# Feed-forward activations and memory outputs 128 bytes further in SBUF

## The chip, the core and the metric

The kernel runs on one core of a Trainium2 chip. The metric is the device time of one execution in microseconds, as the median of several runs. The traces show one profiled execution each.

## What is computed

A sequence of 256 tokens with 1024 features goes through two layers of one kind and one layer of another. All of it is in float32.

```
for l in range(2):                                   # first kind
    h = hybrid_mixer(x, ...)                         # three branches, gated, merged, @ w_mix_out
    x = layer_norm(alpha * x + h, ...)
    h = memory_cross_attention(x, mem, ...)          # softmax(q k) v, then  o @ xa_o
    x = layer_norm(alpha * x + h, ...)
    u, gt = split(x @ ffn_w_in)                      # 1024 -> 2 x 2816
    h = (silu(dwconv(gt, w) + b) * u) @ ffn_w_out    # 2816 -> 1024
    x = layer_norm(alpha * x + h, ...)
# second kind, once
x = x + rms_norm(merged @ w_o)
h = rms_norm(x)
z = conv_b + causal_conv(h @ w_up)                   # both halves, 3 taps
x = x + rms_norm((silu(gate) * val) @ w_down)
```

## The kernel before

Every dense product is done with three matmuls in a 32-bit format with shortened mantissa (`F32R`). A value is split into a high part and the rest: hi x hi, hi x lo and lo x hi are added up in PSUM. So each activation and each weight lies in SBUF twice, as `..._hi` and `..._lo`.

**Weights** come as one stream of 525 halves of 128 x 1024 floats. A half is loaded by DMA into a ring of 5 (`raw_weights`). The scalar or vector engine copies it into `weights_hi` (ring of 4 halves), and the vector engine makes `weights_lo` as the difference (lines 1166 and 1622). A half holds four tiles of 256 columns. TensorE waits for `weights_lo` of a half before it uses it.

**Matmuls.** `linear` (line 601) goes over `kcs` chunks of 128 features. For each chunk it issues six matmuls: two halves of the output by the three products of parts. It has two shapes. With `feature_major` (line 621) the 128 x 128 tile loaded into the array is a weight tile, and the activations, 256 columns, stream. Without it (line 625) the loaded tile is 128 tokens of the activations, and 256 columns of weights stream. Each matmul has a weight load of its own (rows with LDWEIGHTS), which runs beside the matmul ahead of it.

**Feed-forward.** `ffn` (line 964) goes over 11 pairs of feature chunks. For each pair it makes "gt" and "up" (two calls of `linear` with `xT`, line 621, 96 matmuls together), and then, one pair behind, `down_product` (line 639, matmuls in line 663): 48 matmuls in which a tile of `ffn_act` is loaded and 256 columns of the weights stream. They add up over all pairs in four PSUM banks whose names in the trace are `scores`, `probs_transposed` and `attention_out`. The order on TensorE is gt and up of pair 0 and 1, product 0, pair 2, product 1, and so on, then product 9 and product 10. The order is written out by hand; all engines follow it with semaphores. The vector engine writes `ffn_act_hi` and `ffn_act_lo` (lines 1989 and 1632) once per pair, into two slots in turn.

**Memory outputs.** `memory_out` (`XO`) holds the heads' outputs of the cross attention for the product with `xa_o` (line 1059 and 1061, shape of line 625: 4 calls in each of the two layers). The last layer uses the same place for its normalised low-rank inputs (lines 1103 to 1107), streamed 3 x 4 and 2 x 2 chunks, loaded in 24 matmuls.

**Places in SBUF.** One arena is cut by hand; `place` holds the start of each part. `attention_area` is one part in which tiles of different stages overlap. Added up from the sizes in the list, in bytes from the arena's start: weight halves begin at multiples of 4096, `xT_hi` at 70080, `memT_hi` at 102848, `attention_area` at 163136. Each chunk of an activation is 1024 bytes long, each loaded tile 512 bytes. `SHIFT` is 32 floats, 128 bytes. Modulo 512 the weight tiles are on 0, and `xT`, `memT` and `second_branch` on 448. `first_branch`, `third_branch` and `merged`, which have `SHIFT` in their place, are on 448 too (`merged` on 960 modulo 1024), and `ffn_act` and `memory_out`, which do not, on 320.

Of the kernel before, what the change touches and what calls it, by code (L numbers as in the profile page):

```python
# [22 lines left out]
F32R = mybir.dt.float32r  # L23
# [6 lines left out]
T = 256  # L30
# [19 lines left out]
SHIFT = 32  # L50
# [186 lines left out]
def build(nc, a, out):  # L237
    stage = Stage()
    ctx = ExitStack()
    with ctx:  # L240
# [21 lines left out]
        def sb(name, cols, where=None, col0=0, dt=F32):  # L262

            return nc.alloc_sbuf_tensor_at(name, [P, cols], dt, offset=place[where or name] + 4 * col0)
# [16 lines left out]
        area = sb("attention_area", 48 * T + SHIFT, "area")  # L281
        ya_hi, ya_lo = (sb(f"first_branch_{k}", 4 * T, "area", c + SHIFT, F32R) for k, c in (("hi", 0), ("lo", 4 * T)))
        yc_hi, yc_lo = (sb(f"third_branch_{k}", 4 * T, "area", c + SHIFT, F32R) for k, c in (("hi", 28 * T), ("lo", 32 * T)))
        fa_hi, fa_lo = (sb(f"ffn_act_{k}", 4 * T, "area", c, F32R) for k, c in (("hi", 0), ("lo", 4 * T)))
        mg_hi, mg_lo = (sb(f"merged_{k}", 8 * T, "area", c + 128 + SHIFT, F32R) for k, c in (("hi", 8 * T), ("lo", 16 * T)))
        xo_hi, xo_lo = (sb(f"memory_out_{k}", 8 * T, "area", c, F32R) for k, c in (("hi", 24 * T), ("lo", 32 * T)))
        rows = area[:, 40 * T + SHIFT:48 * T + SHIFT]
        stat = sb("softmax_stats", 24, "stat")
        nst = sb("norm_stats", 112, "nst")
# [2261 lines left out]
```

## Time and profile before

| what | value |
|---|---|
| median of 3 runs | 1636.07 us (1635.97 to 1636.3) |
| span of the profiled execution, first to last instruction | 1634.2 us |
| TensorE busy, matmuls | 1620.2 us in 13642 |
| vector engine busy | 1155.2 us |
| scalar engine busy | 868.8 us |
| data moved by DMA | 305.85 MB, 187 GB/s on the mean |
| matmuls of line 621 with `xT` | 3 x 2432 |
| matmuls of line 663 with `ffn_act` | 3 x 528 |
| matmuls of line 625 with `memory_out` | 3 x 136 |

How to read it: matmuls overlap in the array, so one that lasts 276 ns starts about 113 ns after the one before it. The busy time says that TensorE has always something in flight; the rate is read from starts, or from the chain of work, which lists merged runs with their length. The granted TensorE clock is at its upper level, 2.4 GHz, through the whole span.

### The profile page before, as it was taken

Reading aid. Unit: us, or ns where it says so; the run is one execution under the profiler, and the core shown is the slowest. Engines: PE = TensorE matmul, PEld = TensorE weight load, DVE = VectorE, ACT = ScalarE, POOL = GpSimd, SP = SyncE. Lnnn points to the kernel's source line nnn. Section 1 sums busy time; section 2 is a strip of 40 time slices with the busy share of each in tenths; the row PEclk is TensorE's granted clock in tenths of the full one; section 3 lists DMA queues with packets and bytes.
Section 4 is the critical chain, followed back from the end, with each engine's and each line's share of the span. In section 5 each row is a group of like instructions: output and inputs, shape, how many; then the busy total and the mean of one; then the engine's idle time right before and its main releaser. Section 6 shows DMA issues by size and latency. Waiting matters only on the chain.

```text
span 1634.2 us, 32191 instructions
## 1 busy us (share of the span) xinstructions
PE 1620.2 (99%) x13642; PEld 1584.0 (97%) x13642; DVE 1155.2 (71%) x1730; ACT 868.8 (53%) x1305; POOL 40.5 (2%) x59
## 2 busy tenths in 40 slices
PE   9999999999999999999999999999999999999998
PEld 9999999999999999999999999999999999999998
DVE  6588778658666767977974866568576545877777
ACT  5456544646444454555355644455755555464554
POOL 3030000000000000000000000000000000000000
PEclk9999999999999999999999999999999999999999
DMA  9984456535656564445564465655454453556562
GB/s 313 305 213 155 149 197 248 194 130 187 209 173 206 168 238 168 161 149 188 201 234 160 151 227 178 207 173 186 163 173 168 155 180 132 192 168 207 173 204 102
DMA packets 83071, 305.85 MB, mean 187 GB/s; under 512 B 10704, under 2 KB 10832, under 8 KB 80752
## 3 DMA queue, kind: packets, MB, share of 16 engines
q1 hardware_dynamic: 77280, 279.44, 50.1%
q0 software_dynamic: 5648, 24.35, 5.0%
q8 instruction: 108, 1.77, 0.4%
q14 instruction: 35, 0.29, 0.1%
HBM read 300.52 MB, written 6.29 MB: 188 GB/s over the span
## 4 chain that ended last, share of the span: by engine, by line
PE 90%; DVE 7%; issue 1%; ACT 1%; DMA 0%; SPq 0%; DVEq 0%; ACTq 0%
PE general L621 56%; PE general L625 14%; PE scores L663 5%; PE attention_out L663 3%; PE probs_transposed L663 3%; DVE weights_lo L1622 2%; PE attention_out L815 2%; PE scores L748 1%; PE probs_transposed L767 1%; PE scores L839 1%; ACT weights_hi L1166 1%; DVE x_tok L1696 1%; DVE x_tok L1693 1%; DVE xT_lo_part L1632 1%; PE attention_out L859 1%
## 5 line engine op out<-in xcount | busy, mean ns | idle before, releaser
L1622 DVE TENSOR_TENSOR weights_lo<-raw_weights,weights_hi 128x1024 fp32r<-128x1024 f32 x525 | 633.4, 1222 | 372.0 <-ACT weights_hi L1166 369.4
L1166 ACT ACTIVATE weights_hi<-raw_weights 128x1024 fp32r<-128x1024 f32 x525 | 553.2, 1058 | 390.6 <-PE general L621 219.0
L621 PE MATMUL general<-xT_hi_part,weights_hi 128*128 128x256 f32 x2432 | 683.4, 281 | 2.3 <-DVE weights_lo L1622 2.0
L621 PE MATMUL general<-xT_lo_part,weights_hi 128*128 128x256 f32 x2432 | 674.8, 277 | 0.0
L621 PE MATMUL general<-xT_hi_part,weights_lo 128*128 128x256 f32 x2432 | 674.7, 277 | 0.0
L621 PEld LDWEIGHTS general<-xT_hi_part,weights_hi 128*128 128x128 f32 x2432 | 457.4, 188 | 10.5 <-issue 8.8
L621 PEld LDWEIGHTS general<-xT_lo_part,weights_hi 128*128 128x128 f32 x2432 | 457.2, 188 | 1.4 <-issue 1.0
L621 PEld LDWEIGHTS general<-xT_hi_part,weights_lo 128*128 128x128 f32 x2432 | 458.0, 188 | 0.0
L1965 DVE SCALAR_TENSOR_TENSOR exp_ring<-general,param_cols,exp_ring 128x255 f32<-128x255 f32 (+1 forms) x176 | 76.8, 478 | 46.2 <-ACT exp_ring L1362 44.7
L1362 ACT ACTIVATE exp_ring<-general,param_cols 128x256 f32<-128x256 f32 x88 | 44.9, 561 | 69.6 <-PE general L621 69.6
L625 PE MATMUL general<-weights_hi,xT_hi_part 128*128 128x256 f32 x272 | 76.6, 281 | 0.0
L625 PE MATMUL general<-weights_hi,xT_lo_part 128*128 128x256 f32 x272 | 75.8, 279 | 0.0
L625 PE MATMUL general<-weights_lo,xT_hi_part 128*128 128x256 f32 x272 | 75.7, 278 | 0.0
L663 PE MATMUL scores<-weights_hi,ffn_act_hi 128*128 128x256 f32 x264 | 74.1, 281 | 0.8 <-DVE weights_lo L1622 0.8
L663 PE MATMUL scores<-weights_lo,ffn_act_hi 128*128 128x256 f32 x264 | 74.2, 281 | 0.0
L663 PE MATMUL scores<-weights_hi,ffn_act_lo 128*128 128x256 f32 x264 | 74.2, 281 | 0.0
L1177 ACT ACTIVATE attention_area<-general 128x512 f32<-128x512 f32 x60 | 35.7, 595 | 66.4 <-PE general L621 44.1
L1222 ACT ACTIVATE exp_ring<-exp_ring,softmax_stats 128x256 f32<-128x256 f32 (+2 forms) x56 | 28.9, 517 | 67.5 <-DVE softmax_stats L1811 67.4
L625 PEld LDWEIGHTS general<-weights_hi,xT_hi_part 128*128 128x128 f32 x272 | 51.0, 188 | 0.2 <-DVE xT_lo_part L1654 0.2
L1222 ACT ACTIVATE exp_ring<-scores,softmax_stats 128x256 f32<-128x256 f32 x56 | 26.0, 471 | 47.2 <-DVE softmax_stats L1811 47.2
L625 PEld LDWEIGHTS general<-weights_lo,xT_hi_part 128*128 128x128 f32 x272 | 51.1, 188 | 0.0
L625 PEld LDWEIGHTS general<-weights_hi,xT_lo_part 128*128 128x128 f32 x272 | 51.0, 188 | 0.0
(328 smaller groups left out, 2947.4 us busy)
## 6 DMA issues: line engine op xcount, KB each, us to landing
raw_weights<-in_stream SPq DMA_DIRECT2D x525, 512.0 KB, 4.2
attention_area<-in_ln_rows POOLq DMA_DIRECT2D x9, 1024.0 KB, 5.2
bias_scratch<-in_rpb POOLq DMA_DIRECT2D x32, 96.0 KB, 10.5
attention_area<-bias_scratch POOLq DMA_DIRECT2D x2, 1536.0 KB, 8.9
memT_hi<-memT_scratch POOLq DMA_DIRECT2D x2, 1024.0 KB, 5.0
memT_lo<-memT_scratch POOLq DMA_DIRECT2D x2, 1024.0 KB, 8.8
attention_area<-in_mem SPq DMA_DIRECT2D x2, 512.0 KB, 6.0
z_tok<-in_x SPq DMA_DIRECT2D x1, 1024.0 KB, 10.5
```

What stands on the lines that cost most here:

```text
L621: ins = nc.tensor.matmul(ps[b][0:m, half * T:half * T + T], w[wk][:, half * m:half * m + m], x[xk_], start=first, stop=last, skip_group_ch ...
L625: ins = nc.tensor.matmul(ps[b][:, half * T:half * T + T], x[wk][:, half * P:half * P + P], w[xk_], start=first, stop=last, skip_group_chec ...
L663: ins = nc.tensor.matmul(down[2 * t + c][:, q * TILE_N:q * TILE_N + TILE_N], act[xk_][:, kc, t * P:t * P + P], w[wk][:, at:at + TILE_N], s ...
L748: ins = nc.tensor.matmul(dst[:, lo:hi], q, k, start=(c == 0), stop=(c == len(pairs) - 1))
L767: ins = nc.tensor.transpose(tp[:, kt * T + t * P:kt * T + t * P + P], e[:, kt * P:kt * P + P], ident)
L815: ins = nc.tensor.matmul(po[r0:r0 + m, c * T + lo:c * T + T], v, p[:, lo:T], start=first, stop=(g == parts - 1 and kt == 1))
L1166: nc.scalar.activation(hi_half(h), raw_half(h), ACT.Copy).then_inc(*hi_done.more())
L1177: nc.scalar.activation(dst, src[:, :].rearrange("p (c w) -> p c w", w=T), func, **kw).then_inc(*read(key))
L1222: ins = nc.scalar.activation(e, src, ACT.Exp, bias=st("nm", j, t, t + 1), scale=scale if name not in ("na", "mla") else 1.0, accum_out=st( ...
L1362: ins = nc.scalar.activation(cbuf(i % 2, k)[:, c * T:c * T + T], src[:, c * T:c * T + T], ACT.Identity, bias=colp(b, ch, packed), scale=co ...
L1622: nc.vector.tensor_tensor(lo_half(h), raw_half(h), hi_half(h).bitcast(F32), ALU.subtract).then_inc(*lo_done.more())
L1965: ins = nc.vector.scalar_tensor_tensor(d, s, colp(w, 3 * ch + tap, packed), d, ALU.mult, ALU.add)
```

## The change

Two pairs of tiles get `SHIFT` added to their column in `attention_area`: `ffn_act_hi` and `ffn_act_lo`, and `memory_out_hi` and `memory_out_lo`. No instruction, wait or transfer is added, removed or moved. Modulo 512 both pairs are then on 448. `ffn_act` ends 128 bytes further, still ahead of `merged`, and `memory_out` ends where `rows` begins.

```diff
-        fa_hi, fa_lo = (sb(f"ffn_act_{k}", 4 * T, "area", c, F32R) for k, c in (("hi", 0), ("lo", 4 * T)))
+        fa_hi, fa_lo = (sb(f"ffn_act_{k}", 4 * T, "area", c + SHIFT, F32R) for k, c in (("hi", 0), ("lo", 4 * T)))
         mg_hi, mg_lo = (sb(f"merged_{k}", 8 * T, "area", c + 128 + SHIFT, F32R) for k, c in (("hi", 8 * T), ("lo", 16 * T)))
-        xo_hi, xo_lo = (sb(f"memory_out_{k}", 8 * T, "area", c, F32R) for k, c in (("hi", 24 * T), ("lo", 32 * T)))
+        xo_hi, xo_lo = (sb(f"memory_out_{k}", 8 * T, "area", c + SHIFT, F32R) for k, c in (("hi", 24 * T), ("lo", 32 * T)))
```

## Rows read from the trace of the kernel before

**Rows 1.** The page: span, busy time of the engines, engines' shares of the chain.

```profile
span 1634.2 us, 32191 instructions
...
PE 1620.2 (99%) x13642; PEld 1584.0 (97%) x13642; DVE 1155.2 (71%) x1730; ACT 868.8 (53%) x1305; POOL 40.5 (2%) x59
...
PE 90%; DVE 7%; issue 1%; ACT 1%; DMA 0%; SPq 0%; DVEq 0%; ACTq 0%
```

**Rows 2.** Groups of matmuls: streamed tile, loaded tile, count | busy us, mean ns.

```profile
L621 PE MATMUL general<-xT_hi_part,weights_hi 128*128 128x256 f32 x2432 | 683.4, 281 | 2.3 <-DVE weights_lo L1622 2.0
...
L625 PE MATMUL general<-weights_hi,xT_lo_part 128*128 128x256 f32 x272 | 75.8, 279 | 0.0
...
L663 PE MATMUL scores<-weights_hi,ffn_act_lo 128*128 128x256 f32 x264 | 74.2, 281 | 0.0
...
L625 PE MATMUL general<-weights_hi,merged_hi 128*128 128x256 f32 x176 | 48.6, 276 | 0.0
...
L625 PE MATMUL general<-weights_hi,memory_out_lo 128*128 128x256 f32 x136 | 37.7, 277 | 0.0
```

**Rows 3.** Waits of TensorE in the whole run: total us, times, longest.

```profile
PE general L621 <- DVE weights_lo L1622: 2.6, 5, 1.0
```

**Rows 4.** Chain in order of time, one product and block: start us, length us, count.

```profile
425.38 1.41 PE scores L663 x12
426.80 0.71 PE probs_transposed L663 x6
427.50 0.71 PE attention_out L663 x6
428.21 10.90 PE general L621 x96
```

**Rows 5.** Chain in order of time, entry into the first down product.

```profile
394.89 11.11 PE general L621 x98
406.00 1.41 PE scores L663 x12
```

**Rows 6.** Matmuls with `ffn_act_hi` from 1623.5 us: duration ns min/median/max, first, last.

```profile
L663 PE MATMUL scores<-weights_hi,ffn_act_hi x7: 276/276/279, 1623.4 to 1625.5; 128*128 128x256 f32 x7
...
L663 PE MATMUL attention_out<-weights_hi,ffn_act_hi x4: 276/276/276, 1627.2 to 1628.2; 128*128 128x256 f32 x4
```

**Rows 7.** Chain in order of time, other changes from line 621 to 625.

```profile
1185.98 0.91 PE general L621 x8
1186.88 2.83 PE general L625 x24
...
257.91 5.56 PE general L621 x49
263.47 24.49 PE general L625 x216
...
35.98 22.26 PE general L621 x189
58.24 10.83 PE general L625 x92
```

**Rows 8.** Chain in order of time, changes from line 625 to 621.

```profile
354.94 15.64 PE general L625 x138
370.58 2.84 PE general L621 x24
...
1317.08 5.66 PE general L625 x48
1322.74 5.47 PE general L621 x48
...
1133.24 12.98 PE general L625 x108
1146.22 18.84 PE general L621 x160
```

**Rows 9.** Vector engine in order of time: a write of `ffn_act_lo`; start us, length us.

```profile
421.08 0.69 DVE L1632 TENSOR_TENSOR ffn_act_lo<-exp_ring,ffn_act_hi 128x512 fp32r<-128x512 f32 x1
```

## The prediction

> **What bounds the kernel now.** I read the page first: TensorE is busy 1620.2 of 1634.2 us, and it carries 90% of the chain that ended last [rows 1]. Then its waits: in the whole run the largest releaser, the vector engine's `weights_lo`, costs the products of line 621 2.6 us in five waits [rows 3], and the wait view of the first feed-forward stretch (405 to 566 us) names nobody that TensorE waited for. So inside the feed-forward stage the time is the number of matmuls times the spacing between two of them, and no weight or activation comes late. Every matmul there has its own weight load, which runs beside the matmul ahead of it.
>
> The spacing has two values. The chain lists merged runs of matmuls with start and length, so length over count is the spacing. Inside a feed-forward block the 96 matmuls of "gate" and "up" take 10.90 us, 113.5 ns each; the 48 of a down product take 2 x 1.41 + 4 x 0.71 = 5.66 us, 117.9 ns each [rows 4]. I call them fast and slow; the difference is 4.4 ns. The mean duration in the groups shows the same by another number: 276 ns in a fast stretch, 281 in a slow one. Down products against `ffn_act` have 281, projections against `merged` 276, and `memory_out` 277 [rows 2].
>
> I use two shapes below. **F** (line 621): the activations stream and the weights are loaded. **K** (lines 625, 663, 955): the weights stream and the activations are loaded. Offsets are bytes modulo 512 from the arena's start, added up from the sizes: weight halves 0, `xT`, `memT`, branches and `merged` 448, `ffn_act` and `memory_out` 320.
>
> **Does the offset make it slow?** Not alone. The last down product of the run, after its wait, has a median of 276 ns with `ffn_act` at 320 [rows 6]. And K with `xT` at 448 has a mean of 279 [rows 2], and 48 such matmuls from 1317.08 us take 5.66 us, the slow spacing, with the target offset [rows 8]. Fast and slow are states: once in one, a stretch of one shape stays in it over dozens or hundreds of matmuls, and it changes at a wait or at a change of shape. So I look at changes of shape without a wait.
> - Fast F into K at 320: slow. 11.11 us for 98 (113.4 ns), then 1.41 for 12 (117.5) [rows 5]. All 30 entries into the down products look so. `memory_out`, streamed and then loaded, also goes from 0.91 us for 8 (113.8) to 2.83 for 24 (117.9) [rows 7].
> - Fast F into K at 448: stays fast. Branches into `merged`: 5.56 us for 49, then 24.49 for 216, both 113.4 [rows 7]; three such places. Slow F into K at 448 stays slow: 22.26 us for 189 (117.8), then 10.83 for 92 (117.7) [rows 7]; two places.
> - Slow K at 320 into F: fast, at all 27 places between down products and the next block [rows 4].
> - Fast K into F: slow. 15.64 us for 138 (113.3), then 2.84 for 24 (118.3) [rows 8]; both places where it occurs, with `memory_out` loaded ahead and `memT` (448, as `xT`) streamed after.
> - Slow K at 448 into F: fast at three places, the 48 of 1317.08 us followed by 48 in 5.47 us (114.0) as the shown one; at one it stays slow: 12.98 us for 108, then 18.84 for 160 (117.8) [rows 8].
>
> **The change, part by part.** It adds, removes and moves no instruction, wait or transfer; three tile addresses change their base by 128 bytes. The vector and scalar engines write the same shapes; I cost that at nothing, since the vector engine is idle 29% of the span and nothing on TensorE's side waits for it inside the stage. The writes of `ffn_act` end about 0.6 us before their product starts (421.08 + 0.69 us against 422.4) [rows 9], so 128 bytes either way would have to lengthen a write by half before TensorE waits; a slower block only widens that gap.
>
> Down products. A block order is: gate and up of pairs 0 and 1, product 0, block 2, product 1, ..., block 10, products 9 and 10. Today, per layer, the 11 products are slow (528 matmuls) and all blocks after the first are fast. After the change product 0 is entered from a fast block and should stay fast (branches into `merged`). Then comes the step that matters: leaving a fast K. The weight load of the next block then runs beside a matmul at the fast timing, as in rows 8, and there the F stretch went slow. So block 2 is slow, product 1 stays slow (rows 7), and leaving it gives fast again (3 of 4). The pattern has a period of two blocks: of 288 matmuls 144 are slow, against 96 now. Counted out per layer: slow blocks after products 0, 2, 4, 6, 8 (5 x 96 = 480) and slow products 1, 3, 5, 7, 9, 10 (6 x 48 = 288), 768 in place of 528. 240 x 3 layers x 4.4 ns = 3.2 us longer.
>
> Memory outputs. They are loaded in 408 matmuls of line 625 in all. At 277 in place of 276 ns about one in five is slow now. After restarts K at 448 is mostly slow (mean 279 against `xT`, [rows 2]); if `memory_out` becomes like that, 3 in 5, some 160 to 200 more are slow, 0.7 to 0.9 us; the two groups of 48 that follow the output projections without a wait would then go from slow to fast, 0.4 back. Net 0.5, between 0 (nothing changes) and 1.4 (all slow). The 96 matmuls that stream `memory_out` in the last block cannot hold more than 0.4 either way.
>
> Sum: 3.2 + 0.5 = 3.7 us on a span of 1634.2. What lies around the span, 1.9 us (median 1636.1 less span), stays. **1639.8 us.**
>
> What the Trainium skill says on this ("SBUF — State Buffer", section Operand start alignment): an operand only has to begin at a multiple of its element size, and the page adds that its runs timed nothing. By it alone 320 and 448 would be alike; that is case E below. The spacing itself, by "TensorE: Matmul & The Clock Gate" (section Back-to-back issue gap), is set by the weight load and the matmul together; the rows agree so far as the two states differ in this pair, 113.5 and 117.9 ns, but that page has nothing about two states or addresses.
>
> **The rivals.**
> - B, faster: the F stretch after a fast product stays fast. Its place is the 27 exits from down products, and it decides there alone: for it speaks that no exit from a fast K at 448 into F is in the trace (after the projections against `merged` comes another K), and that both fast exits seen are from 320. Against it: at that moment the loaded tile is a weight half at offset 0 and no activation is loaded any more, so the 448 should not matter. Then nearly all of the 1584 product matmuls turn fast; some 40 at the end already are: 1540 x 4.4 ns = 6.8 us less, with memory outputs 0.5 more: 1629.8.
> - C, no difference: `ffn_act` is entered slow at 448 too. For it: the entry from `memory_out` to itself had equal offsets and went slow, and `ffn_act` against `xT` would have equal offsets as well; `merged` differs from the branches by 512 bytes. Exits stay as today. Only the 0.5 stays: 1636.6.
> - D, slower still: exits from a slow K at 448 keep the slow state (1 in 4). Then all nine blocks after product 0 are slow too: 9 x 96 x 3 = 2592 matmuls x 4.4 ns = 11.4 us, 1648.
> - E, the change does not do what it says: the states have nothing to do with the offset, and it comes out at 1636.1.
>
> **How the numbers follow.** A 0.38, B 0.24, C 0.20, D 0.09, E 0.09. A mixture, with some exits that stay slow, would lie between A and D. The range takes in A, B, C, E with the bounds of the memory outputs and leaves D: 1628.5 to 1644. A's own range is 1638.2 (only two thirds of the blocks, memory 0) to 1644. What a measurement can tell from no change is about 0.2%, 3.3 us, so faster means below 1632.8 and slower above 1639.3. Faster: B, 0.24. Same: C, E and the low end of A, 0.20 + 0.09 + 0.05 = 0.34. Slower: the rest of A and D, 0.42.
>
> **What would show it.** In the groups, `ffn_act` matmuls split between 276 and 281 ns with a mean near 278 to 279 (A), all 276 (B), all 281 (C, D). In the chain of one layer, blocks of 96 that alternate between 10.9 and 11.3 us (A), all 10.9 (B, C), all 11.3 (D). The mean of `xT` in line 621 should rise by about 1 ns in A, as 1440 of its 7296 matmuls turn slow. The first product of each layer tells the entry step, the block behind it the exit step. TensorE's waits should be as now; if instead its waits for `weights_lo` grow, the supply of weights had no room for the faster stage and B's gain is smaller. What would make the prediction wrong is mainly the exit step, which rests on two places, and an entry step that rests on three with another distance between the tiles.

## The result

The changed kernel takes 1638.72 us (median of 21 runs, 1637.21 to 1640.01) against 1636.07 (21 runs, 1632.55 to 1637.75): ratio 1.0017, 95% interval 1.001 to 1.0023. It is slower by 2.7 us; the interval leaves out 1, so the direction stands. The forecast was 1639.8, slower by 3.7. By the forecast's own limit for calling a kernel slower, 1639.3 us, the result still counts as no change. The profiled execution has a span of 1637.5 us, 3.3 more than before.

The page of the changed kernel, the lines that answer to [rows 1]:

```profile
span 1637.5 us, 32191 instructions
...
PE 1622.9 (99%) x13642; PEld 1586.6 (97%) x13642; DVE 1155.8 (71%) x1730; ACT 869.2 (53%) x1305; POOL 40.6 (2%) x59
```

The groups that answer to [rows 2]: `xT` in line 621, `ffn_act`, `merged`, `memory_out`.

```profile
L621 PE MATMUL general<-xT_lo_part,weights_hi 128*128 128x256 f32 x2432 | 676.7, 278 | 0.0
L663 PE MATMUL scores<-weights_hi,ffn_act_lo 128*128 128x256 f32 x264 | 73.3, 278 | 0.0
L625 PE MATMUL general<-weights_hi,merged_lo 128*128 128x256 f32 x176 | 48.6, 276 | 0.0
L625 PE MATMUL general<-weights_hi,memory_out_lo 128*128 128x256 f32 x136 | 37.9, 279 | 0.0
```

`ffn_act` went from 281 to 278 ns: the products became faster, as the offset seems to promise. `xT` in the blocks between them rose (277 to 278 over 2432 matmuls of this kind), `memory_out` from 277 to 279, `merged` did not move. The chain in order of time, layer 0, two rounds of product and block, answering to [rows 4] (start us, length us, count):

```profile
429.03 11.31 PE general L621 x96
...
445.99 10.89 PE general L621 x96
456.89 1.36 PE scores L663 x12
458.25 0.68 PE probs_transposed L663 x6
458.93 0.68 PE attention_out L663 x6
459.61 1.36 PE scores L663 x12
460.97 0.68 PE probs_transposed L663 x6
461.65 0.68 PE attention_out L663 x6
462.33 11.31 PE general L621 x96
473.64 1.42 PE scores L663 x12
```

The block at 445.99 us is fast (113.4 ns), so is the product behind it (2 x 1.36 + 4 x 0.68 = 5.44 us, 113.3 ns), the next block is slow (11.31 us, 117.8 ns) and the product behind that too. This is the period of two blocks from the forecast. Read block by block from starts of matmuls, every block and product of all three layers follows it, but for one exit in layer 1 that stayed slow: the one behind that layer's first product, at 960.20 us.

### The profile page after: what moved, and what is told of

It reads as the page before. It is cut to its first block, busy times and chain, and to the rows that moved or that the text cites. A ratio compares the mean times of both kernels' runs of the same rounds, so it can differ in the third digit from the quotient of the medians.

```text
span 1637.5 us, 32191 instructions
## 1 busy us (share of the span) xinstructions
PE 1622.9 (99%) x13642; PEld 1586.6 (97%) x13642; DVE 1155.8 (71%) x1730; ACT 869.2 (53%) x1305; POOL 40.6 (2%) x59
## 4 chain that ended last, share of the span: by engine, by line
PE 89%; DVE 7%; ACT 2%; issue 1%; DMA 0%; SPq 0%; DVEq 0%; ACTq 0%
PE general L621 56%; PE general L625 14%; PE scores L663 5%; PE attention_out L663 2%; PE probs_transposed L663 2%; DVE weights_lo L1622 2%; PE attention_out L815 2%; PE scores L748 1%; PE probs_transposed L767 1%; ACT weights_hi L1166 1%; PE scores L839 1%; DVE x_tok L1696 1%; DVE x_tok L1693 1%; DVE xT_lo_part L1632 1%; PE attention_out L859 1%
```

## The experiments

Each kernel was compared with the kernel before on the same chip. "Fast" and "slow" are the 113.4 and 117.8 ns spacings, F streams activations (line 621), K loads them (lines 625 and 663). Offsets are from the arena's start. In e3 to e12 `memory_out` stays on 320.

**Each half of the change alone.**

```diff
 # e1_ffn_only
-        fa_hi, fa_lo = (... "area", c, F32R) ...
+        fa_hi, fa_lo = (... "area", c + SHIFT, F32R) ...
 # e2_mem_only
-        xo_hi, xo_lo = (... "area", c, F32R) ...
+        xo_hi, xo_lo = (... "area", c + SHIFT, F32R) ...
```

> Only ffn_act moves by 128 bytes, memory_out stays on 320. Theory (states pass through the change of shape; a product at 448 keeps the state it is entered in, leaving a fast product makes the next block slow, leaving a slow one makes it fast): the feed-forward blocks alternate as in the changed kernel, chain rows of 96 matmuls at 10.9 and 11.3 us in turn, ffn_act mean 278 ns, about +3 us against the kernel before, so nearly all of the change's loss. Rival (the loss comes from memory_out and from the stages behind it): under +1 us.

Measured: 1638.01 us, ratio 1.0012 (1.0003 to 1.0021); the medians lie 1.6 us apart, the ratio says 2.0. The alternation is there, chain of its trace:

```profile
428.19 11.31 PE general L621 x96
...
445.16 10.89 PE general L621 x96
456.05 1.36 PE scores L663 x12
```

> Only memory_out moves, ffn_act stays on 320. Theory: feed-forward as before (ffn_act 281 ns, blocks of 96 all 10.9 us), memory_out 279 ns in place of 277, between 0 and +1.4 us. Rival (memory_out carries the loss): +2 us or more.

Measured: 1636.43 us, ratio 1.0004 (0.9995 to 1.0013). `memory_out` has 279 ns, the products keep 281:

```profile
L663 PE MATMUL scores<-weights_hi,ffn_act_lo 128*128 128x256 f32 x264 | 74.1, 281 | 0.0
L625 PE MATMUL general<-weights_hi,memory_out_lo 128*128 128x256 f32 x136 | 37.9, 279 | 0.0
```

So most of the loss is the feed-forward stage, and the memory outputs add what cannot be told from zero. The traces say the same: from the first to the last matmul of line 663 the three stages together are 2.3 us longer than before in e1, as in the changed kernel, and equal to before within 0.01 us each in e2. The 279 ns alone prove little for `memory_out`: it has the same mean in e3, e4 and e12, where it was not moved. Here too the other half of the forecast's term shows: the 24 matmuls behind the last output projection take 2.75 us (114.6 ns) in place of 2.84 [rows 8], since leaving a slow K gives a fast F.

**How far the offset counts.**

```diff
 # e3_ffn_plus512: 320 modulo 512, 832 modulo 1024
+        fa_hi, fa_lo = (... "area", c + 4 * SHIFT, F32R) ...
 # e4_ffn_plus640: 448 modulo 512, 960 modulo 1024, as merged
+        fa_hi, fa_lo = (... "area", c + 5 * SHIFT, F32R) ...
 # e8_ffn64: 64 modulo 512
+        fa_hi, fa_lo = (... "area", c + 2 * SHIFT, F32R) ...
```

> ffn_act moves by 512 bytes: still 320 modulo 512, but another offset modulo 1024. If only the offset modulo 512 counts: all products slow, all blocks behind them fast, the time of the kernel before within 0.5 us. If the period is longer (1024 or more), entries or exits differ from before and the stage shows another pattern.

> ffn_act moves by 640 bytes: 448 modulo 512 and 960 modulo 1024, exactly where merged lies. If only modulo 512 counts: the alternation of the changed kernel, about +3 us. If modulo 1024 counts: another pattern, up to all fast (-7 us) should the exit from 960 keep the fast state.

> Only ffn_act moves, to 64 modulo 512 (256 bytes further than before). Theory: entry at distance 64 turns slow or keeps slow, exits from slow products turn fast, so the pattern and time of the kernel before (0 to +0.5 us). Rival (320 is the one bad offset): alternation as with 448, +3 us.

Measured: e3 1637.01 us, ratio 1.0005 (0.9995 to 1.0014); e4 1638.88, ratio 1.0017 (1.0008 to 1.0026); e8 one run of 1635.88 beside a median of 1635.88. The chains of e3, e4 and e8, in this order:

```profile
429.02 10.90 PE general L621 x96
439.93 1.41 PE scores L663 x12
```

```profile
428.03 10.89 PE general L621 x96
438.93 1.36 PE scores L663 x12
```

```profile
428.18 10.90 PE general L621 x96
439.08 1.41 PE scores L663 x12
```

At 320 and 832 a fast block is followed by a slow product (1.41), at 448 and 960 by a fast one (1.36). And 64 behaves as 320. So for the loaded activation the offsets that were tried fall into two classes modulo 256: 64 (offsets 64, 320, 832) and 192 (offsets 448, 960). My rival of a longer period falls, and "320 is the one bad offset" falls too.

**Moving what streams.** I held that the distance of loaded and streamed tile decides. The next kernels move `xT` instead. Its two tiles go behind everything else, with a gap that sets the offset; all other tiles keep theirs modulo 512.

```diff
-                 ("x", 2 * D), ("z", 2 * D), ("xT_hi", 2 * D), ("xT_lo", 2 * D), ("keep", 2 * D), ("big", 24 * T),
+                 ("x", 2 * D), ("z", 2 * D), ("keep", 2 * D), ("big", 24 * T),
-                 ("stat", 24))
+                 ("stat", 24), ("gap", 8), ("xT_hi", 2 * D), ("xT_lo", 2 * D))
```

The gap is 8 floats for `xT` on 64 and 24 for 128. The expectation of e10 says 0 modulo 512, but its gap of 56 is 192 bytes more than that of e5, so `xT` lies on 256 modulo 512, which is 0 modulo 256. `ffn_act` has `+ SHIFT` in e5, e9 and e10 (448), nothing in e6 (320), `+ 2 * SHIFT` in e7 (64).

> xT_hi and xT_lo lie behind everything else, on 64 modulo 512 in place of 448; ffn_act on 448; all other tiles keep their offset modulo 512. Theory (what counts is the distance loaded minus streamed: at 448, as with merged, a disturbed start falls back to the fast state, at 320 and 64 it turns slow): streaming xT at 64 with weights loaded at 0 has the distance 448, so leaving a fast product leaves the next block fast. All blocks of 96 at 10.9 us, and if the entry holds too all products at 5.4 us; -7 us or more, since other stretches with xT (7296 matmuls, 2000 slow before) turn fast as well. Rival (only the absolute offset of the loaded activation counts): blocks alternate as in the first experiment, +3 us.

> xT on 64, ffn_act on 320 as before. Theory: blocks all fast; the entry into the products has the distance 320 and turns slow or, if the exit and entry distances matter in another way, not: products 281 ns, about the kernel before or some us less by the other stretches with xT. Rival (offset of xT without effect): the kernel before within 0.1%.

> xT on 64, ffn_act on 64. Theory: in the products the distance loaded minus streamed is 64, the one that blocks with xT at 448 have now, at which a disturbed start turns slow. So blocks fast, products slow where the entry disturbs. Between the two other kernels with xT on 64.

Measured: e5 1659.43 us, ratio 1.014 (1.0123 to 1.0157); e6 1648.43, ratio 1.0076 (1.0061 to 1.0091); e7 1648.62, ratio 1.0078 (1.0063 to 1.0093). The theory of the distance predicted a gain and got the largest loss so far: it falls. In the chain of e5 everything is slow:

```profile
434.68 11.31 PE general L621 x96
445.98 1.41 PE scores L663 x12
```

In e6 (and the same in e7) the products turn the state over and the blocks keep it: a slow block gives a fast product (1.37), that one a fast block (10.88), and a fast block a slow product:

```profile
430.22 0.71 PE probs_transposed L663 x6
430.93 0.71 PE attention_out L663 x6
431.63 11.31 PE general L621 x96
442.94 1.37 PE scores L663 x12
...
447.71 0.68 PE attention_out L663 x6
448.40 10.88 PE general L621 x96
```

That answers the disputed step. With `xT` on 448 leaving a product turns the state over, with `ffn_act` on 320, 64, 448 or 960 (27 exits in each trace, one exception, in the changed kernel; fast exits occur only with 448 and 960). With `xT` on 64 leaving keeps it, with `ffn_act` on 448, 320 or 64 (27 exits in each trace; all start slow in e5, both states occur in e6 and e7). The same traces hold a check: behind the last product of the first feed-forward stage `memT` streams, which kept its 448, and there e5, e6 and e7 turn from slow (117.8 ns) to fast (113.3). What the exit does goes with the streamed tile that comes; no dependence on the activation that was loaded is seen. And e6 and e7 agree, which is the period of 256 again.

> xT on 128 modulo 512, ffn_act on 448. The distance rule has fallen (xT on 64 made 6600 matmuls slow). Theory now: whether a stretch that streams xT starts fast after a wait or an exit depends on the offset of xT modulo 256 against the weights' 0; 192 is good after waits (7 in 10 fast) and toggles at exits, 64 is bad after waits and keeps at exits. 128 is untried: if it lies between, some 3000 to 5000 slow matmuls with xT and +3 to +10 us. If 128, furthest from 0, is free of the effect, all blocks at 10.9 us and -10 us or more.

> xT on 0 modulo 512, the offset of the weights. If equal offsets of loaded and streamed tile are what disturbs (as at an exit, where a weight tile at 0 is loaded beside another one that streams), every stretch with xT is slow or slower still: +20 us or more. If the period of 256 with 192 good and 64 bad is a matter of who is ahead, 0 lies between: +3 to +15 us.

Measured: e9 1671.94 us, ratio 1.0223 (1.0205 to 1.0242); e10 1670.61, ratio 1.0215 (1.0199 to 1.0231). Neither bound of e9 held (+10), and e10 has the loss that its first theory named (+20 or more). It does not prove that theory: `xT` is on 256 and has the weights' offset only modulo 256, and e9, without equal offsets, loses as much. In e10 blocks take 11.52 us, 120 ns, a third and slower spacing, and all products behind them are fast:

```profile
435.45 11.52 PE general L621 x96
446.96 1.36 PE scores L663 x12
448.32 0.68 PE probs_transposed L663 x6
449.00 0.68 PE attention_out L663 x6
```

```profile
L663 PE MATMUL scores<-weights_hi,ffn_act_lo 128*128 128x256 f32 x264 | 72.9, 276 | 0.0
```

With `xT` on 128, 26 of the 27 blocks take 11.39 us, a mean of 118.6 ns over single spacings that go round between 115 and 122:

```profile
436.24 11.39 PE general L621 x96
```

So of the four placements of `xT` tried, the one of the kernel before, on 448, is the best, by 12 us or more. In e5 the projections against `merged`, whose tiles did not move, went from 276 to 279 ns, because the branches before them were already slow:

```profile
L625 PE MATMUL general<-weights_hi,merged_lo 128*128 128x256 f32 x176 | 49.1, 279 | 0.0
```

That `merged` at 448 is fast in the kernel before is inherited, and no merit of its offset alone.

**Moving the low weights.** They change places with a small tile.

```diff
-("w_lo", SPLIT * HALF_N), ("nst", 112),
+("nst", 112), ("w_lo", SPLIT * HALF_N),
```

> weights_lo moves to 448 by changing places with a small tile behind it; every other tile keeps its offset modulo 512, ffn_act on 448. Theory: a third of the matmuls load or stream weights_lo, so the offsets now change inside a stretch, every third matmul. If a change of offsets is what can toggle the state, it does so all the time: the spacing inside stretches becomes mixed (durations between 276 and 281) and branches and merged, all fast so far, lose it; +10 us or more. Rival (the offset of the loaded or streamed weights is without effect): alternation and +3 us as with ffn_act on 448 alone.

Measured: 1670.0 us, ratio 1.0213 (1.0197 to 1.0229). The blocks have the slow spacing, the products a still slower mean, 118.9 to 119.0 ns by their starts:

```profile
436.12 11.30 PE general L621 x96
447.42 1.43 PE scores L663 x12
```

The offset of the weights counts too; that stretches no longer hold the fast spacing is what I expected, its single steps I did not take apart.

**Something between product and block.**

```diff
                     if i:
                         down_product(i - 1)
+                    if 0 < i < FPAIR - 1:
+                        keep_busy(1)
```

> ffn_act on 448 (memory_out on 320, xT on 448), and one small matmul (128 columns, constants by constants) between a down product and the block behind it, 9 in each layer, 27 in all. It costs about 0.11 us each (transposes against constants follow one another at 0.109 us), 3 us in all. Theory: the alternation comes from the exit, where a weight tile is loaded beside streaming weights; with another matmul in between, the block starts as behind transposes, and then its state no longer depends on the product's. If it starts fast each time, all blocks are at 10.9 us and all products at 5.4 us: 3.0 - 7.0 = -4 us against the kernel before. If it starts slow each time: all blocks at 11.3 us, all products slow, +3 + 11 = +14 us. Rival (the state belongs to the pair index or to the weights, not to the exit): alternation stays as it is and only the cost is added, +3 + 2 = +5 us.

Measured: 1652.52 us, ratio 1.0103 (1.0086 to 1.012), +16.6 us.

```profile
412.89 0.22 PE general L694 x2
413.11 11.31 PE general L621 x96
424.43 1.42 PE scores L663 x12
...
430.08 0.22 PE general L694 x2
430.30 11.31 PE general L621 x96
```

The alternation is gone: each of the 27 blocks starts slow, behind 25 products at the slow spacing and 2 at the fast, and `ffn_act` at 448 then keeps slow. The stage is 5.5 to 5.7 us longer in each of the three layers. The rival (state bound to the pair or to the weights) would have kept the alternation, and falls. The call leaves two matmuls in the trace and costs 0.22 us and not 0.11, 6 us in all, which is the miss of 2.6 us against the +14 of the expectation's slow branch.

## Why the prediction held, and where its sizes were off

**The bound.** Right. TensorE's waits for `weights_lo` in line 621 are 3.7 us in eight, beside 2.6 in five [rows 3], all of them outside the blocks and products, but for the one of line 663 ahead of the last product:

```profile
PE general L621 <- DVE weights_lo L1622: 3.7, 8, 1.0
PE scores L663 <- DVE weights_lo L1622: 1.0, 1, 1.0
```

**Entry into a product at 448.** Right: the state is kept, in 30 of 30 entries, 14 fast and 16 slow. C rested on the objection that equal offsets (as with `memory_out` to itself, [rows 7]) or the 512 bytes between `merged` and `ffn_act` could spoil it; e4, which has the offset of `merged`, and the change itself agree, so C falls.

**Exit from a fast product.** Right, and this step decided the sign: all 12 such exits between product and `xT` block turned slow. B, the natural hope behind the offset, falls with it. The argument, that at this moment no activation is loaded any more, fits the exits of e5 to e8, where only the offset of the streamed tile changes what happens.

**Exit from a slow product at 448.** Fast in 14 of 15 places, not 3 of 4; so D does not happen.

**The count.** Here a term was mis-sized: the slow matmuls that each layer gains. I took each layer to enter its first product fast, for 240 more slow matmuls a layer. In the profiled execution all three entered slow, as the first row of layer 0's chain shows beside [rows 5]:

```profile
389.83 17.20 PE general L621 x144
```

144 matmuls in 17.20 us are 119.4 ns each, with a restart at the head; without it, by the starts, 117.8, where [rows 5] have 113.4. Layers 0 and 2 then have 624 slow matmuls (4 blocks, 5 products), layer 1 has 816 (5 blocks and 7 products, by its one exit that stayed slow): 2064 in place of some 1540, about 2.3 us at 4.4 ns. From the first to the last matmul of line 663 the three stages are 0.34, 1.19 and 0.75 us longer, 2.28 in all, by the starts in both traces, against 3.2 predicted. Where a layer does enter fast, as the first two in e4 do, it is 0.98 us longer, near the 1.06 of the sum; the rest is that fewer exits are paid for: a turn from slow to fast costs some 20 ns in its first four matmuls, and half of the 27 are gone.

**Outside the stage.** The rest of the span grew by 1.1 us, 0.5 was predicted, with 1.4 as the upper bound. Read from the starts of the same matmuls in both traces, this is a sum of larger terms:

- The matmuls that load `memory_out` take 1.3 us more. By the starts 370 of the 408 are slow, 67 before, more than the three of five I took. The two groups behind the output projections give back 0.2 us each, as predicted. So the memory outputs cost 0.9 us net in these two traces, 0.5 was predicted. How much of it is the offset stays open: with `memory_out` left on 320, 71 are slow in e1 and 52 in e8, but 216, 224 and 209 in e3, e4 and e12.
- The stretches just ahead of the three first products take 0.8 us more each, 2.5 us in all, being slow here and fast before (0.2 us of it is a longer wait in each of the first two layers).
- Everything else is 2.3 us shorter, mostly other stretches that were slow before and are fast here.

The last two terms are in no sum of the forecast, and they nearly cancel. That the two profiled spans differ by 3.3 us, so close to the 3.7, is partly luck. The slow first blocks need not come from the change: e1 has the same row at 389.00 us, with no moved tile used before that place, and e8, whose stage runs as in the kernel before, has it too:

```profile
388.77 17.20 PE general L621 x144
```

In the first two layers they follow a wait for the weights (0.33 us just ahead of 389.83), and after such a wait both states occur: in layer 0 e1 goes on slow and the kernel before fast, both behind a gap of 0.42 us between two starts. Which state a stretch starts in thus differs from trace to trace. It is a likely reason why runs of one kernel spread over 3 to 5 us here, and why the 2.7 us of the medians and the 3.3 of the two profiled spans differ; no experiment isolates it.

E, that the state has nothing to do with the offset, is refuted by the changed kernel, by e1 and e4, and by each kernel in which `xT` or `weights_lo` moved. Placements that are all in order by the Trainium skill ("SBUF — State Buffer", section Operand start alignment) lie 2.2% apart here; that section speaks of what is allowed, and the measurement decides on the speed.

**What stays open.** The runs give the table of which offsets keep and which turn the state, not the mechanism that makes it. A version with the products fast and the blocks fast was not found: with `xT` on 448 each exit from a fast product turns slow, and no other offset of `xT` was better as a whole. In e5, e6, e7, e9 and e10 `xT` also lies some 126000 bytes further on, and `xT` on 448 in that new place was not run. That the offset counts rests there on the differences between these kernels, with `ffn_act` on 448 1659.4 us for 64, 1671.9 for 128 and 1670.6 for 256, and on `memT`, which moved by 16384 bytes and behaves as before. `xT` on 0 modulo 512 was not tried. Activation offsets between the classes for `ffn_act` (0 and 128 modulo 256) were not tried.

## What to carry to other kernels

A tile that "runs slow" may only have inherited a state from the stretch before it: look at the change of shape where the state turns before moving the tile, and count what the next stretch gets. Here the moved tile became faster (281 to 278 ns) and handed the slow spacing to a stretch twice as long. Judge such a change by the spacing of the whole round, product and block, not by the group of the tile that moved.

## What the runs showed of the hardware

- A stream of weight load and matmul pairs (128 x 128 loaded, 256 columns, `F32R`) has at the same granted clock (0.999 in the traces of the kernel before, the changed kernel and e10) at least three stable spacings: 113.4, 117.8 and 120 ns. Uneven ones lie between, 118.6 ns on the mean in e9 and 118.9 in e11. Which one holds depends on the SBUF offsets of loaded and streamed tile and on the state before.
- The offsets of the loaded activation that were tried act alike when they agree modulo 256: 64 and 320 and 832 (e8, before, e3), 448 and 960 (the change, e4).
- With `xT` on 448 leaving a product turns the state over (80 of 81 exits with `ffn_act` on 448 or 960: the change, e1, e4), with `xT` on 64 it is kept (81 of 81: e5, e6, e7). Entering at 448 from `xT` at 448 keeps it (30 of 30), entering at 64, 320 or 832 from there always gives slow (30 of 30 each in the kernel before, e3 and e8), entering at 64 or 320 from `xT` at 64 turns it over (30 of 30 each in e6 and e7).
- The whole range over these placements of the same instructions is 1635.9 to 1671.9 us, 2.2%.
